# Sample attention beside expert lookups: VectorE's and ScalarE's stages set one pair of slots behind TensorE's, weights turned a stage later, joining products in another bank

## Chip, core and metric

The kernel is one program on one core of a Trainium2 chip. The metric is the device time of one execution in microseconds (us), the median over the runs. Names: TensorE (PE, its weight loads PEld), VectorE (DVE), ScalarE (ACT), GpSimd (POOL), SyncE (SP).

## What is computed

One inference step of a decoder of two layers, for a prompt of 512 rows and for eight sample rows that attend to a past of 4096 rows each. All is float32. Layer 0's first half is a convolution and a gated linear attention, layer 1's is multi-head latent attention; both layers end with an expert lookup (PEER). What matters here, cut from the reference:

```python
def odd_layer(x, pos, ckv_past, kpe_past, ...):       # layer 1: latent attention
    z = rms_norm(x, norm_g) @ w_in
    c_q, c_kv, k_pe = jnp.split(z, [R_Q, R_Q + R_KV], axis=-1)
    ...
    sp = (einsum('bqhr,bkr->bhqk', ql, ckv_past)      # sample rows: 8 sequences, 4096 past rows
          + einsum('bqhd,bkd->bhqk', qp, kpe_past)) * MLA_SCALE
    p = softmax(concatenate([sp, s], axis=-1))
    o = (einsum('bhqk,bkr->bqhr', p[..., :n_past], ckv_past) + einsum(... p[..., n_past:], ckv))
    ...
def peer(h, w_q, sub_keys, u_tab, v_tab):             # both layers: 8 heads, 16 experts of each
    q = (xf @ w_q).reshape(n, H_P, 2, D_HALF)
    s_top, i_top = top_k(einsum('nhcd,hckd->nhck', q, sub_keys), TOPK)
    ... ids, gates = the 16 best sums of pairs, their softmax
    act = gelu(einsum('td,thkd->thk', xb, u_tab[ib])) * gb
    return einsum('thk,thkd->td', act, v_tab[ib])
```

`ckv_past` is (8, 4096, 256) and `kpe_past` (8, 4096, 32), read from a paged cache through `page_table`.

## The kernel before, in words

**Expert slots.** `peer_layer` handles 512 (head, expert) slots of 128 rows in each layer, and eight more of the sample rows. For a slot GpSimd gathers 128 rows of 8 KB (line 1177) into one of `RING` = 8 buffers, VectorE forms the dot of each row's first half with the normalised input (`dot`, line 1569), ScalarE the gelu, the product with the gate and a diagonal matrix (`weigh`, lines 1297, 1299, 1303), and TensorE adds the row's second half, weighted by the diagonal, to `acc` (`experts`, line 1782). Then the buffer is free for the slot eight further on. Slots go in pairs (`GROUP` = 2), and eight pairs (`GROUPS`) make one head n of `NW` = 32. Between the pairs of a head each engine has the routing of head n + 2: queries before the head's first pair on TensorE (line 1717, for half of the heads), scores after its second and third (line 1727), their copies on ScalarE, the top-k on VectorE behind the dots of pairs 3 to 6.

**Attention beside them.** The latent attention of layer 1 is spread over both lookups, since its work fits between slots. It is written as generators, one per engine: `latent_round` for the prompt rows, then `sample_round` for the sample rows (sequences 0 and 1 beside layer 0's lookup, 2 to 7 beside layer 1's). Each engine chains the two and, at the end of every pair of slots, takes one step (`next(steps, None)`, lines 1147, 1197, 1408, 1663, 1834), in layer 0 from head 14 on, in layer 1 up to head 27; what is left runs after the last pair. So stage s of the attention stands, on every engine, behind the same pair's slot work. Engines are bound to each other by semaphores alone and each executes its list in order. `latent_round` has 93 stages in layer 0 and 101 in layer 1; the sample round has 51 and 118.

**A piece.** The past of a sequence is read in four pieces of 8 x 128 rows (1.18 MB). A piece p begins a new stage every four (`piece_at(s, offset)`). Its stages, with the engine's line: offset -2 the gather on GpSimd (line 2527, into one of three page buffers, after the weighted products of piece p - 3); 0 and 1 TensorE turns two quarters of the pages each (`turn_pages`, line 2802: left in bank 0, right in bank 1), ScalarE copies the left (line 2570) and the last right part (line 2574), VectorE the first right part (`page_out`, line 2653); 2 the rotary part (lines 2824 and 2578); 3 the scores (`scores`, lines 2850 and 2854, in bank 2), their maximum (`maxima`, line 2665) and exponentials (`exps`, lines 2583 and 2584); 4 the weights turned (`turn_weights`, line 2860, in bank 2) and copied (`weights_out`, line 2590); 5 the weighted products (`weighted`, line 2869, in bank 2) and their sum (`add_piece`, lines 2681 and 2688). Stage 4 of a piece is stage 0 of the next.

**Joins.** After a sequence's last piece four short steps join the partial sums: `turn_top`, `spread_top`, `total_sums` and `fold_heads` on TensorE (lines 2874, 2880, 2887, 2893) with `largest`, `shares`, `weighed_sum`, `normed` and `folded` (line 2720) on the others. They are four stages apart while pieces follow and one apart at the end of a round. Their products go to bank 2, which `scores` of the next piece may enter only once they are read (its last four waits). At layer 0's end VectorE adds `acc` to x (line 1584) behind the last pair.

Of the kernel before, what the change touches and what calls it, by code (L numbers as in the profile page):

```python
# [953 lines left out]
GROUP = 2  # L954
# [11 lines left out]
def peer_layer(nc, w, layer, ident, x_sb, smp, out):  # L966
# [11 lines left out]
    with ExitStack() as ctx:  # L978
# [81 lines left out]
        assert att["stages"] <= GROUPS * (NW - ROUND_AT if layer == 0 else PAIR_NORM)  # L1060
        assert att["stages"] + smp_att["stages"] <= GROUPS * (NW - ROUND_AT if layer == 0 else SMP_X)
        block = ctx.enter_context(nc.Block())
# [40 lines left out]

        def hooked(n):
            return n >= ROUND_AT if layer == 0 else n < SMP_X

        @block.sync
        def _(sp):
# [16 lines left out]
            for n in range(-AHEAD, NW):  # L1125
                i = head_of(n + AHEAD)
                for g in range(GROUPS):
                    if g == 4 and i is not None and n + AHEAD < NW and i + HEADS_IN < NQ_HEADS:
                        sp.wait_ge(s_ps, score_no(n + AHEAD + H_P) + 1)
                        if with_sample(i):  # L1130
                            sp.wait_ge(smp_s_ps, i % H_P + 1)
                        load_head(i + HEADS_IN)
                    if last_layer and n == SMP_X - 1 and g == 4:
                        sp.wait_ge(s_ps, score_no(NW - 1) + 1)
                        load_head(NQ_HEADS)
                        load_head(NQ_HEADS + 1)
                    if last_layer and n == SMP_X and g == 1:
                        sp.wait_ge(smp_att["done"], 1)
                        for h in range(HEADS_IN, H_P - 1):
                            w_dst, k_dst = smp_head(h)[0:2]  # L1140
                            sp.dma_start(w_dst, w["w_q_heads"][layer, :, h]).then_inc(smp_w_in, 16)
                            sp.dma_start(k_dst.rearrange("p c n -> p (c n)"), w["keysT"][layer][:, D_KEY * h:D_KEY * h + D_KEY]).then_inc(smp_w_in, 16)
                    if last_layer and n == SMP_HEADS and g == 2:
                        sp.wait_ge(smp_s_ps, 1)
                        sp.dma_start(w_q[:, 0], w["w_q_heads"][layer, :, H_P - 1]).then_inc(w_q_in[0], 16)
                        sp.dma_start(keys[:, 0].rearrange("p c n -> p (c n)"), w["keysT"][layer][:, D_KEY * (H_P - 1):D_KEY * H_P]).then_inc(w_q_in[0], 16)
                    if n >= 0 and hooked(n):
                        next(steps, None)
# [14 lines left out]
        def _(pool):  # L1163
# [22 lines left out]
            for n in range(NW):  # L1186
# [6 lines left out]
                for k in range(TOPK):  # L1193
                    if n == 0 and k == 8:
                        pool.wait_ge(routed, 1)
                    gather(first_slot(n) + k, ids[:, n % (AHEAD + 1), k:k + 1])
                    if hooked(n) and k % GROUP == GROUP - 1:
                        next(steps, None)
# [4 lines left out]
        def _(act):  # L1203
# [154 lines left out]
            for n in range(NW):  # L1358
# [6 lines left out]
                for g in range(GROUPS):  # L1365
# [40 lines left out]
                    if g == 6 and m < NW:  # L1406
                        exps(route_no(m))
                    if hooked(n):
                        next(steps, None)
# [9 lines left out]
        def _(dve):  # L1419
# [197 lines left out]
            for n in range(NW):  # L1617
# [6 lines left out]
                for g in range(GROUPS):  # L1624
# [26 lines left out]
                    if m < NW:  # L1651
# [9 lines left out]
                        if g == 6 + late:  # L1661
                            lookup(route_no(m), ids[:, m % (AHEAD + 1), :])
                    if hooked(n):
                        next(steps, None)
# [11 lines left out]
        def _(pe):  # L1676
# [125 lines left out]
            for n in range(NW):  # L1802
# [6 lines left out]
                for g in range(GROUPS):  # L1809
# [22 lines left out]
                    if (n, g) == SPREAD_PE[1]:  # L1832
                        smp_spread_x(1)
                    if hooked(n):
                        next(steps, None)
# [556 lines left out]
def sample_round(nc, ctx, w, out, ident, x_sb, smp, rnd, att):  # L2392
# [6 lines left out]
    LAST_AT = SETUP + 4 * (NPC - 1)  # L2399
    OUT_AT = LAST_AT + 11  # L2400
    STAGES = LAST_AT + 10 if rnd == 0 else OUT_AT + 7

# [54 lines left out]
    s_cols, o_cols = banks[2][:, 0:256], banks[2][:, 256:256 + R_KV]  # L2457
    top_row, bias_col, total_col, fold_out = banks[2][0:1, 0:128], banks[2][:, 0:1], banks[2][:, 0:1], banks[2][:, 0:2 * H_C]

# [8 lines left out]
    def merge_stage(i, step):  # L2468

        last = PAST_PIECES * i + PAST_PIECES - 1  # L2470
        return SETUP + 4 * last + 6 + step * (4 if last + 1 < NPC else 1)

# [5 lines left out]

    def outs_before(i, step):

        return min(PAST_PIECES * i + PAST_PIECES + step, NPC)

# [7 lines left out]
    def sync_steps(sp):  # L2490
# [10 lines left out]
        for s in range(STAGES):  # L2501
# [8 lines left out]
            if rnd == 1 and s == LAST_AT + 4:  # L2510
                sp.wait_ge(s_ps, NPC)
                sp.dma_start(w_uv, w["c_w_uv"][0].rearrange("(k p) h n -> p k (h n)", p=128)).then_inc(uv_in, 16)
            if rnd == 1 and s == LAST_AT + 6:
                sp.wait_ge(o_ps, NPC)
# [30 lines left out]
    def scalar_steps(act):  # L2545
# [46 lines left out]
        def shares(i):  # L2592
# [6 lines left out]
            nc.scalar.activation(share[:, 1:2], new_top(PAST_PIECES * i + PAST_PIECES - 1), ACT.Exp, bias=share[:, 0:1], scale=MLA_SCALE).then_inc(share_ready, 1)  # L2599

        for s in range(STAGES):
            if rnd == 0 and s == 6:
# [3 lines left out]
            if rnd == 0 and s == 8:  # L2606
                latent_queries_out()
            if (p := piece_at(s, 4)) is not None:
                weights_out(p)
# [16 lines left out]
    def vector_steps(dve):  # L2626
# [95 lines left out]
        def add_out():  # L2722
# [4 lines left out]
            last.then_inc(y_used, 1)  # L2727

        for s in range(STAGES):
            if rnd == 0 and s == 6:  # L2730
# [3 lines left out]
            if rnd == 0 and s == 9:  # L2734
                self_out()
            if (p := piece_at(s, 5)) is not None:
                add_piece(p)
# [18 lines left out]
    def tensor_steps(pe):  # L2756
# [48 lines left out]
        def turn_pages(p, r):  # L2805
# [10 lines left out]
            elif p:  # L2816
                pe.wait_ge(right_act, p)
            turn_page(banks[1], p, 4 * r + 2, right_ps)

# [7 lines left out]
        def scores(p):  # L2827
# [7 lines left out]
            elif rnd == 0:  # L2835
                pe.wait_ge(self_ready, 1)
            if p >= PAST_PIECES:
                i, step = divmod(p - PAST_PIECES, PAST_PIECES)
                if step == 0:
                    pe.wait_ge(mx_ready, i + 1)  # L2840
                if step == 1:
                    pe.wait_ge(bias_out, i + 1)
                if step == 2:
                    pe.wait_ge(inv_step, 2 * i + 1)
                if step == 3:
                    pe.wait_ge(olT_ready, i + 1)
            b = ROUND_SEQS[p // PAST_PIECES]
# [24 lines left out]
        def turn_top(i):  # L2872
            pe.wait_ge(o_used, outs_before(i, 0))
            nc.tensor.transpose(top_row, new_top(PAST_PIECES * i + PAST_PIECES - 1), ident[:]).then_inc(topT_ps, 1)

        def spread_top(i):
            pe.wait_ge(consts, 1)
            pe.wait_ge(nmx_ready, i + 1)
            pe.wait_ge(o_used, outs_before(i, 1))
            nc.tensor.matmul(bias_col, nmx[:].rearrange("p j h -> p (j h)"), one[:], start=True, stop=True).then_inc(bias_ps, 1)  # L2880

        def total_sums(i):
            pe.wait_ge(lw_ready, i + 1)
            pe.wait_ge(bias_out, i + 1)
            pe.wait_ge(consts_in, 48)
            pe.wait_ge(o_used, outs_before(i, 2))
            nc.tensor.matmul(total_col, fold[:], share[:, 2:3], start=True, stop=True).then_inc(total_ps, 1)

        def fold_heads(i):
            pe.wait_ge(on_ready, i + 1)  # L2890
            pe.wait_ge(o_used, outs_before(i, 3))
            for c in range(2):
# [22 lines left out]
        for s in range(STAGES):  # L2915
# [11 lines left out]
            if (p := piece_at(s, 2)) is not None:  # L2927
                turn_rope(p)
            if (p := piece_at(s, 4)) is not None:
                turn_weights(p)  # L2930
            if (p := piece_at(s, 5)) is not None:
                weighted(p)
# [127 lines left out]
```

## Time and profile before

| | us |
|---|---|
| median of 3 runs | 3596.35 (3595.26 to 3619.91) |
| the profiled execution | 3605.23 |
| its span, first to last instruction | 3603.4 |
| PE / DVE / ACT / POOL busy in the span | 2576.4 / 2175.5 / 1593.2 / 1195.2 |
| mean granted TensorE clock | 0.816 of full speed |
| moved | 1240.70 MB, mean 344 GB/s |

A row of the profile gives a line of the kernel, the engine, what it writes and reads, its duration, and in brackets how long the engine was idle before it and what released it. A wait is put down to what came last. Layer 0's lookup runs up to about 1846 us, layer 1's from about 1890 us.

### The profile page before, as it was taken

The page shows a single profiled execution, that of the slowest core. Times are in us where ns is not written, and L with a number is a line of the kernel's source. Part 1 is how long each engine was busy: PE and PEld are TensorE (multiplying, and loading weights), DVE is VectorE, ACT ScalarE, POOL GpSimd, SP SyncE. Part 2 cuts the span into 40 slices and gives each one's busy share as a digit, 9 for nine tenths or more (in the row PEclk, how much of TensorE's full clock was granted, in tenths as well). Part 3 has the DMA queues.
Part 4 walks back from the last instruction along what each step waited for, and adds up shares of the span by engine and source line. Part 5 has one row for each costly group of instructions (what it writes and reads, how often), then busy time and mean ns, then how long its engine had stood idle before and what let it go on. Part 6 is the DMA issues. An engine that isn't in the chain of part 4 may idle for free. (4 is left out here: it accounts for less than half of the span.)

```text
span 3603.4 us, 44291 instructions
## 1 busy us (share of the span) xinstructions
PE 2576.4 (71%) x15271; PEld 1136.2 (32%) x15271; DVE 2175.5 (60%) x5407; ACT 1593.2 (44%) x4435; POOL 1195.2 (33%) x1114
## 2 busy tenths in 40 slices
PE   8987776666788875766656888866767666656566
PEld 7644222111334432322232443422323322221121
DVE  4863667767776776545345778866454454455566
ACT  3122444444555663244433557744444444444344
POOL 0210444444443443333213344433222222222343
PEclk9988776766898997776777999988888778776687
DMA  4115999999999999898759999999888788888998
GB/s 158 46 32 190 411 426 426 422 427 427 418 400 421 422 420 396 359 370 308 278 214 384 408 421 421 423 406 368 328 330 302 288 309 304 294 295 314 417 426 362
DMA packets 215854, 1240.70 MB, mean 344 GB/s; under 512 B 28015, under 2 KB 63503, under 8 KB 72773
## 3 DMA queue, kind: packets, MB, share of 16 engines
q0 software_dynamic: 154368, 1128.34, 77.5%
q1 hardware_dynamic: 59965, 108.63, 8.2%
q8 instruction: 121, 1.98, 0.2%
q10 hardware_dynamic: 1296, 0.90, 0.1%
q14 instruction: 104, 0.85, 0.1%
HBM read 1233.79 MB, written 4.46 MB: 344 GB/s over the span
## 5 line engine op out<-in xcount | busy, mean ns | idle before, releaser
L1782 PE MATMUL p_acc<-p_rows,p_diag 64*64 64x512 f32 x8192 | 1390.5, 791 | 865.7 <-ACT p_diag L1303 850.3
L1177 POOL DMA_INDIRECT p_rows<-in_peer_uv,p_ids x1024 | 1102.3, 1076 | 2036.6 <-PE p_acc L1782 1886.7
L1569 DVE CUSTOM_DVE_ANT_0 p_rows<-p_rows,p_x_n 128x1024 f32<-128x1024 f32 x1040 | 1248.5, 1221 | 491.6 <-DMA p_rows<-in_peer_uv,p_ids 479.5
L1782 PEld LDWEIGHTS p_acc<-p_rows,p_diag 64*64 64x64 f32 x8192 | 288.3, 159 | 1655.2 <-ACT p_diag L1303 1477.5
L1297 ACT ACTIVATE p_acts<-p_dots 128x1 f32<-128x1 f32 x1040 | 209.2, 201 | 1038.7 <-DVE p_dots L1569 1035.0
L1303 ACT ACTIVATE p_diag<-p_unit,p_gated 128x64 f32<-128x64 f32 x1024 | 356.0, 348 | 33.5
L1299 ACT ACTIVATE p_gated<-p_acts,p_gates 128x1 f32<-128x1 f32 x1024 | 301.7, 295 | 33.3
L1717 PE MATMUL p_q_banks<-p_xT,p_w_q 128*128 128x256 f32 (+3 forms) x1152 | 245.0, 374 | 22.9 <-DMA p_keys<-in_keysT 14.5
L1717 PEld LDWEIGHTS p_q_banks<-p_xT,p_w_q 128*128 128x128 f32 x1152 | 210.1, 204 | 57.9 <-issue 30.9
L1297 ACT ACT_TABLE_LOAD x142 | 182.2, 1283 | 5.9 <-DVE p_dots L1569 3.4
L2665 DVE TENSOR_REDUCE s_peak<-r_bank 128x1 f32<-128x256 f32 x32 | 13.6, 424 | 178.3 <-PE r_bank L2854 178.3
L2653 DVE COPY r_arena<-r_bank 128x512 f32<-128x512 f32 x32 | 22.1, 691 | 145.3 <-PE r_bank L2802 145.3
L2802 PEld LDWEIGHTS r_bank<-ident,r_arena 128*128 128x128 f32 x512 | 81.0, 187 | 71.5 <-issue 71.5
L2688 DVE SCALAR_TENSOR_TENSOR r_arena<-r_arena,s_alpha,r_bank 128x256 f32<-128x256 f32 x32 | 15.4, 480 | 141.3 <-PE r_bank L2869 141.3
L2802 PE MATMUL r_bank<-ident,r_arena 128*128 128x128 f32 x512 | 96.4, 351 | 0.0
L541 DVE SCALAR_TENSOR_TENSOR a_conv<-a_u,a_conv_wc,a_conv 128x512 f32<-128x512 f32 x120 | 86.6, 793 | 0.0
L688 PE MATMUL a_ps<-a_xT,a_w_in 128*128 128x260 f32 x384 | 85.7, 384 | 0.1
L1569 DVE DVE_READ_ACCUMULATOR2_ANT p_dots<- 128x1 f32 x1040 | 84.5, 81 | 0.0
L1289 ACT ACT_TABLE_LOAD x64 | 82.1, 1283 | 1.1
L2355 PE MATMUL r_bank<-r_arena 128*128 128x256 f32 x192 | 52.9, 437 | 41.1 <-DMA r_arena<-in_c_w_out 41.1
L688 PEld LDWEIGHTS a_ps<-a_xT,a_w_in 128*128 128x128 f32 x384 | 72.6, 190 | 11.9 <-issue 0.4
L2570 ACT COPY r_arena<-r_bank 128x512 f32<-128x512 f32 x64 | 37.7, 588 | 83.2 <-PE r_bank L2802 83.1
(417 smaller groups left out, 2787.3 us busy)
## 6 DMA issues: line engine op xcount, KB each, us to landing
p_w_q<-in_w_q_heads SPq DMA_DIRECT2D x35, 1024.0 KB
p_rows<-in_peer_uv,p_ids POOLq DMA_INDIRECT x1024, 14.2
r_arena<-in_c_w_out SPq DMA_DIRECT2D x8, 1024.0 KB, 24.7
a_w_in<-in_ab_w_in SPq DMA_DIRECT2D x6, 1024.0 KB, 11.7
r_arena<-in_w_qx SPq DMA_DIRECT2D x16, 384.0 KB, 12.6
r_arena<-in_c_w_in SPq DMA_DIRECT2D x2, 2688.0 KB, 13.0
r_arena<-in_w_q_heads SPq DMA_DIRECT2D x5, 1024.0 KB, 23.8
p_keys<-in_keysT SPq DMA_DIRECT2D x35, 128.0 KB
```

Of the source, the lines that this page charges most:

```text
L541: ins = nc.vector.scalar_tensor_tensor(out=conv[:, c, 0:SEQ], in0=u[:, c, i:i + SEQ], scalar=conv_wc[:, c, i:i + 1], in1=conv[:, c, 0:SEQ] ...
L688: last = nc.tensor.matmul(ps[bank][:, 512 * b:512 * b + half], w_in[:, k, at:at + 128], xT[:, k, half_of(b)], start=(k == 0), stop=(k == K ...
L1177: nc.gpsimd.indirect_dma_start(out=rows[:, slot % RING, :], out_offset=None, in_=w[f"peer_uv{layer}"], in_offset=bass.IndirectOffsetOnAxis ...
L1289: nc.scalar.activation(ex[:], rel[:], ACT.Exp, accum_out=ex_sum[:]).then_inc(ex_ready, 1)
L1297: nc.scalar.activation(acts[:, i % 4, j:j + 1], dots[:, i % 4, j:j + 1], ACT.Gelu).then_inc(gelud, 1)
L1299: nc.scalar.mul(gated[:, i % 4, j:j + 1], acts[:, i % 4, j:j + 1], gate[:, j:j + 1]).then_inc(gated_ready, 1)
L1303: nc.scalar.mul(diag[:, i % 4, j, 0:n], unit[:], gated[:, i % 4, j:j + 1]).then_inc(diag_ready, 1)
L1569: nc.vector.tensor_tensor_reduce(rows[:, k % RING, 0:D_MODEL], rows[:, k % RING, 0:D_MODEL], x, 1.0, 0.0, ALU.mult, ALU.add, dots[:, slot ...
L1717: last = nc.tensor.matmul(q_banks[:, c, lo:hi], w_q[:, i % HEADS_IN, k, 128 * c:128 * c + 128], xT[:, k, lo:hi], start=(k == 0), stop=(k = ...
L1782: last = nc.tensor.matmul(acc[64 * c:64 * c + 64, 512 * r:512 * r + 512], diag[of, slot // GROUP % 4, j, :], rows[of, (slot + j) % RING, a ...
L2355: last = nc.tensor.matmul(banks[2 * (q % 2) + i][:, 0:256], oT[:, k, 128 * i:128 * i + 128], w_out[:, q % W_SLOTS, k, :], start=(k == 0), ...
L2802: last = nc.tensor.transpose(bank[:, 256 * c + 128 * u:256 * c + 128 * u + 128], past[:, p % PAGES, at:at + 128], ident[:])
```

## The change

In `sample_round`, VectorE's and ScalarE's generators begin with a bare `yield`, so that each of their stages stands one pair of slots behind TensorE's, SyncE's and GpSimd's. The stages from the turned weights on move up by one: weights turned and copied at offset 5, weighted and added at 6, the joins from offset 7 of the last piece. The joins' products go to bank 1 instead of bank 2: they wait for the right pages read (`right_act`) instead of `o_used`, and the right page turn waits for them to be read, instead of `scores`. `turn_top` waits for the maximum itself. `OUT_AT` goes up by one (119 stages in layer 1) and layer 0's round has 53 stages, of which the last two (and three on VectorE and ScalarE) run after the last pair. `hooked` takes a second argument that it does not use.

```diff
-        assert att["stages"] + smp_att["stages"] <= GROUPS * (NW - ROUND_AT if layer == 0 else SMP_X)
+        assert att["stages"] + smp_att["stages"] < (GROUPS * (NW - ROUND_AT) + 4 if layer == 0 else GROUPS * SMP_X)
...
-    OUT_AT = LAST_AT + 11
-    STAGES = LAST_AT + 10 if rnd == 0 else OUT_AT + 7
+    OUT_AT = LAST_AT + 12
+    STAGES = LAST_AT + 12 if rnd == 0 else OUT_AT + 7
...
-    top_row, bias_col, total_col, fold_out = banks[2][0:1, 0:128], banks[2][:, 0:1], banks[2][:, 0:1], banks[2][:, 0:2 * H_C]
+    top_row, bias_col, total_col, fold_out = banks[1][0:1, 0:128], banks[1][:, 0:1], banks[1][:, 0:1], banks[1][:, 0:2 * H_C]
...
-        return SETUP + 4 * last + 6 + step * (4 if last + 1 < NPC else 1)
+        return SETUP + 4 * last + 7 + step * (4 if last + 1 < NPC else 1)
...
-    def outs_before(i, step):
-
-        return min(PAST_PIECES * i + PAST_PIECES + step, NPC)
+    def turned_before(i, step):
+
+        return min(PAST_PIECES * i + PAST_PIECES + 1 + step, NPC)
...
-            if rnd == 1 and s == LAST_AT + 6:
+            if rnd == 1 and s == LAST_AT + 7:
                 sp.wait_ge(o_ps, NPC)
...
+        yield
         for s in range(STAGES):
...
-            if (p := piece_at(s, 4)) is not None:
+            if (p := piece_at(s, 5)) is not None:
                 weights_out(p)
...
+        yield
         for s in range(STAGES):
...
-            if (p := piece_at(s, 5)) is not None:
+            if (p := piece_at(s, 6)) is not None:
                 add_piece(p)
...
             elif p:
                 pe.wait_ge(right_act, p)
+            if r == 0 and p > PAST_PIECES:
+                i, step = divmod(p - PAST_PIECES - 1, PAST_PIECES)
+                if step == 0:
+                    pe.wait_ge(mx_ready, i + 1)
+                if step == 1:
+                    pe.wait_ge(bias_out, i + 1)
+                if step == 2:
+                    pe.wait_ge(inv_step, 2 * i + 1)
+                if step == 3:
+                    pe.wait_ge(olT_ready, i + 1)
             turn_page(banks[1], p, 4 * r + 2, right_ps)
...
-            if p >= PAST_PIECES:
-                i, step = divmod(p - PAST_PIECES, PAST_PIECES)
...
         def turn_top(i):
-            pe.wait_ge(o_used, outs_before(i, 0))
+            pe.wait_ge(top_step, 3 * (PAST_PIECES * i + PAST_PIECES))
+            pe.wait_ge(right_act, turned_before(i, 0))
...
-            pe.wait_ge(o_used, outs_before(i, 1))
+            pe.wait_ge(right_act, turned_before(i, 1))
...
-            if (p := piece_at(s, 4)) is not None:
+            if (p := piece_at(s, 5)) is not None:
                 turn_weights(p)
-            if (p := piece_at(s, 5)) is not None:
+            if (p := piece_at(s, 6)) is not None:
                 weighted(p)
```

`total_sums` and `fold_heads` wait for `right_act` in the same way, with steps 2 and 3.

## Rows read from the trace of the kernel before

**Rows 1.** The page's slices: GB/s in 40 equal slices of the span.

```profile
GB/s 158 46 32 190 411 426 426 422 427 427 418 400 421 422 420 396 359 370 308 278 214 384 408 421 421 423 406 368 328 330 302 288 309 304 294 295 314 417 426 362
```

**Rows 2.** Busy time by stretch: start:end, us, PE, PEld, DVE, ACT, POOL, clock, DMA share, GB/s.

```profile
1550.00:1810.00 260.00, 161.99 (x1081) 59.45 (x1073) 120.96 (x302) 111.38 (x299) 73.68 (x74) 0.73 0.83 314
2070.00:2320.00 250.00, 219.86 (x1310) 106.22 (x1303) 193.35 (x506) 159.39 (x417) 109.09 (x94) 0.96 1.02 421
2535.00:3307.00 772.00, 496.14 (x3480) 219.38 (x3476) 378.63 (x1009) 347.95 (x903) 208.24 (x213) 0.80 0.83 304
```

**Rows 3.** The same, of the dots (line 1569) alone.

```profile
1550.00:1810.00 260.00, 81.63 (x138) 0.73 0.83 314
2535.00:3307.00 772.00, 227.47 (x384) 0.80 0.83 304
```

**Rows 4.** Waits in layer 1's sample attention, then in layer 0's: total us, times, longest.

```profile
DVE s_peak L2665 <- PE r_bank L2854: 136.5, 24, 14.4
DVE r_arena L2653 <- PE r_bank L2802: 107.8, 23, 7.2
DVE r_arena L2688 <- PE r_bank L2869: 96.0, 24, 6.0
...
DVE s_peak L2665 <- PE r_bank L2854: 41.8, 8, 7.5
DVE r_arena L2653 <- PE r_bank L2802: 37.3, 8, 6.2
DVE r_arena L2688 <- PE r_bank L2869: 36.9, 7, 6.2
```

**Rows 5.** Waits in the stretch 2070 to 2320 us.

```profile
DVE p_rows L1569 <- DMA p_rows<-in_peer_uv,p_ids: 42.5, 37, 2.1
```

**Rows 6.** Timeline of one pair of slots, 2769 to 2779 us: start, us, engine, line.

```profile
2769.68 0.69 DVE L2653 COPY r_arena<-r_bank 128x512 f32<-128x512 f32 x1 [3.55 <-PE r_bank L2802]
...
2770.22 0.59 ACT L2570 COPY r_arena<-r_bank 128x512 f32<-128x512 f32 x1
...
2771.43 1.22 DVE L1569 CUSTOM_DVE_ANT_0 p_rows<-p_rows,p_x_n 128x1024 f32<-128x1024 f32 x1
...
2772.51 3.23 PE L1782 MATMUL p_acc<-p_rows,p_diag 64*64 64x512 f32 x16 [2.60 <-ACT p_diag L1303]
...
2778.19 0.48 DVE L2688 SCALAR_TENSOR_TENSOR r_arena<-r_arena,s_alpha,r_bank 128x256 f32<-128x256 f32 x1 [2.64 <-PE r_bank L2869]
```

**Rows 7.** Timeline of TensorE where it has the queries, 2783 to 2805 us.

```profile
2783.36 7.07 PE L1717 MATMUL p_q_banks<-p_xT,p_w_q 128*128 128x256 f32 x32
2790.36 1.95 PE L1782 MATMUL p_acc<-p_rows,p_diag 64*64 64x512 f32 x16
2792.24 1.07 PE L2850 MATMUL r_bank<-r_arena,smp_qlT 128*32 128x256 f32 x16
2793.12 0.62 PE L2854 MATMUL r_bank<-r_arena,s_qpb 128*32 128x128 f32 x16
2797.67 3.69 PE L1782 MATMUL p_acc<-p_rows,p_diag 64*64 64x512 f32 x16 [3.93 <-ACT p_diag L1303]
```

**Rows 8.** Transfers of layer 1's sample attention, then of 2070 to 2320 us.

```profile
DMA packets 33496, 235.01 MB, mean 304 GB/s; under 512 B 3665, under 2 KB 5073, under 8 KB 5626
p_rows<-in_peer_uv,p_ids POOLq DMA_INDIRECT x192, 7.6
r_arena<-in_cache_rows,smp_row_ids POOLq DMA_INDIRECT x21, 9.8
...
p_rows<-in_peer_uv,p_ids POOLq DMA_INDIRECT x94, 15.3
```

**Rows 9.** Timeline of the end of layer 0.

```profile
1842.94 1.03 PE L2893 MATMUL r_bank<-s_fold_h,r_arena 128*128 128x16 f32 x4
1844.01 0.21 DVE L2720 COPY smp_olT<-r_bank 128x32 f32<-128x32 f32 x1 [4.54 <-PE r_bank L2893]
1844.12 2.77 DVE L1584 TENSOR_TENSOR x_sb<-x_sb,p_acc 64x512 f32<-64x512 f32 x4
```

More of the change, by code:

```diff
@@ L1102, in buffer_of, with hooked @@
             return x_n[:, t % 3, :]
-        def hooked(n):
+        def hooked(n, g):
             return n >= ROUND_AT if layer == 0 else n < SMP_X
@@ L1146, in _ @@
                         sp.dma_start(keys[:, 0].rearrange("p c n -> p (c n)"), w["keysT"][layer][:, D_KEY * (H_P - 1):D_KEY * H_P]).then_inc(w_q_in[0], 16)
-                    if n >= 0 and hooked(n):
+                    if n >= 0 and hooked(n, g):
                         next(steps, None)
@@ L1196, in _ @@
                     gather(first_slot(n) + k, ids[:, n % (AHEAD + 1), k:k + 1])
-                    if hooked(n) and k % GROUP == GROUP - 1:
+                    if k % GROUP == GROUP - 1 and hooked(n, k // GROUP):
                         next(steps, None)
@@ L1407, in _ @@
                         exps(route_no(m))
-                    if hooked(n):
+                    if hooked(n, g):
                         next(steps, None)
@@ L1662, in _ @@
                             lookup(route_no(m), ids[:, m % (AHEAD + 1), :])
-                    if hooked(n):
+                    if hooked(n, g):
                         next(steps, None)
@@ L1833, in _ @@
                         smp_spread_x(1)
-                    if hooked(n):
+                    if hooked(n, g):
                         next(steps, None)
@@ L2836, in scores @@
                 pe.wait_ge(self_ready, 1)
-            if p >= PAST_PIECES:
-                i, step = divmod(p - PAST_PIECES, PAST_PIECES)
[L2839 to L2846, printed above, removed]
             b = ROUND_SEQS[p // PAST_PIECES]
@@ L2885, in total_sums @@
             pe.wait_ge(consts_in, 48)
-            pe.wait_ge(o_used, outs_before(i, 2))
+            pe.wait_ge(right_act, turned_before(i, 2))
             nc.tensor.matmul(total_col, fold[:], share[:, 2:3], start=True, stop=True).then_inc(total_ps, 1)
@@ L2890, in fold_heads @@
             pe.wait_ge(on_ready, i + 1)
-            pe.wait_ge(o_used, outs_before(i, 3))
+            pe.wait_ge(right_act, turned_before(i, 3))
             for c in range(2):
```

## The prediction, made before the changed kernel was run

> **What bounds the kernel now.** I read the slices of the page first, then the busy time by stretch, the waits, the transfers, and last a timeline of single steps. The whole program reads 1240.7 MB, and the slices show two levels [rows 1]: 420 to 427 GB/s in the middle of each layer, near 300 in slices 17 to 19 and 28 to 35. The low slices are where the sample attention runs. Its stretch in layer 1 (2535 to 3307 us, 24 pieces) and in layer 0 (1550 to 1810 us, 8 pieces) move 304 and 314 GB/s, the stretch of layer 1 just before, with another attention and the same expert work, 421 [rows 2]. The dots divide these into pairs of slots (each dot is a product and an accumulator read, so four instructions to a pair) [rows 3]: 384 make 96 pairs in 772 us, 8.04 us each; 138 make 34.5 in 260 us, 7.5 each. The fast stretch gathers 94 slots, 47 pairs, in 250 us [rows 8]: 5.3 each. No engine is full in the slow stretches: TensorE has 496 of 772 us, VectorE 379, ScalarE 348 [rows 2]. So latency bounds them, and the waits name it [rows 4]: VectorE waits 136.5 + 107.8 + 96.0 = 340.3 us for TensorE's scores, turned pages and weighted products, and 41.8 + 37.3 + 36.9 = 116.0 us in layer 0; it has no wait for rows near the top of either list. In the stretch before, it waits for the rows' DMA instead, 42.5 us [rows 5]: that is how a stretch looks that the transfers bound.
>
> The timeline shows the ring [rows 6]. The page copy on VectorE waits 3.55 us for turned pages and ends at 2770.4; only then come the two dots (1.22 us each, the second from 2771.43), ScalarE's gelu, gate and diagonal (the experts begin at 2772.51, 1.0 us behind the first dot's end), TensorE's 16 expert products (3.23 us), its turn, and again a copy that VectorE has waited for (2.64 us). TensorE does nothing from the end of one step to the next diagonal (2.60 us). Every engine waits once round the ring, and TensorE, paused so often, is granted 0.80 of its clock here against 0.96 in the fast stretch [rows 2]. The experts' 16 products took 1.95 us straight after seven busy microseconds of queries, and 3.69 us after the next pause of 3.93 us [rows 7], the two levels of 2.4 and 1.2 GHz.
>
> **The bare `yield` on ScalarE and VectorE.** Stage s of the sample attention then stands behind the dots (on ScalarE the gelus) of pair h + 1, where TensorE's stands behind its experts of pair h. It removes no instruction; it takes the wait out of the ring. While TensorE does experts and stage of pair h, VectorE already does the dots of h + 1. VectorE's list would be 772 - 340 = 432 us in layer 1 and 260 - 116 = 144 in layer 0, if each wait went. I checked each consumer on TensorE for a new wait. The bank for the next turn is emptied by ScalarE right behind the gelus of the same pair, a 0.59 us copy [rows 6] beside experts of 1.95 to 3.69 us; VectorE's copy (0.69) stands behind its dots and at most 2.9 us of routing, which end about when the experts do. Scores need the rotary copy of the same pair, likewise covered. VectorE's `add_piece` releases the score bank behind the dots of the pair in which TensorE wants it, 0.7 us against the same cover. If that cover goes, it costs about a microsecond a piece, 32 in all.
>
> **Weights turned and multiplied a stage later.** `exps` now runs on ScalarE a pair later; without the shift TensorE would meet it too early. Same instructions, no cost. But `weighted` frees the page buffer, and the gather of piece p + 3 stands two pairs ahead on GpSimd's queue. GpSimd runs four pairs ahead of the experts (8 row slots), so the gather's wait now falls on exactly the pair in which TensorE does `weighted`. Queued behind it are the row gathers; the next of them needs a slot that the experts after `weighted` free, so it would wait anyway. What stays is the gather's own issue, 1.0 to 1.9 us, at most 1 us late per piece beside a ring of four pairs: 0 on the path, and up to 32 us if rows are the bound with no slack.
>
> **Joins in bank 1.** They move out of the score bank, so `scores` drops its four waits and the right page turn takes them. The largest is step 1: the turn waits for ScalarE's bias copy, behind `exps`, which stands behind VectorE's routing and maxima. About 1.5 us for TensorE, once for each of eight sequences, under VectorE's list: nothing, at most 12 us.
>
> **What is late next.** The transfers. The 772 us stretch moves 235.01 MB [rows 8], at 422 GB/s 557 us, above VectorE's 432 and TensorE's 496 busy (fewer at a better clock). The worst pair, the one with the queries, blocks TensorE for 7.07 + 1.95 + 1.1 + 0.6 = 10.7 us [rows 7], and VectorE then stands at the maxima; but rows in flight (7.6 us to land here, 15.3 where transfers bound [rows 8]) span it. An octet of pairs with queries is then 10.7 us plus seven pairs at 3.5 to 5 (experts of 1.95 to 3.7 and a stage of 1.5), 35 to 46 us; VectorE's own list is 432 / 12 = 36; the transfers of an octet are 557 / 12 = 46. That is near enough that some gaps stay, so I take 400 GB/s rather than 422. Layer 1: 235.01 / 0.400 = 588, a gain of 184 us (bounds: 0, and 215 at 422). Layer 0: 260 x 0.314 = 81.6 MB, / 0.400 = 204, a gain of 56 (0 to 66). The joins at the end of layer 0 (1810 to 1846 us) have four more such waits, the last 4.54 us [rows 9]; half of it gone is 6 (0 to 18). Against that, layer 0 now has 53 stages from pair 93 on in 144, so its last fold and copy come after the last 2.77 us addition: 1.03 + 0.21 [rows 9] and the small norm steps, +2 us (0 to +5). Layer 1's tail keeps its length (-8 to +5, I take 0).
>
> The sum against the profiled execution, 3605.2 us outside a span of 3603.4: 3605.2 - 184 - 56 - 6 + 2 = 3361. It lies 8.9 us above the median of the runs, so the forecast is 3352 us.
>
> One rule speaks against this. The Trainium skill (DMA: Bandwidth & Descriptors, Where 436 GB/s comes from) holds that transfers from HBM are bound by a core's share of the stack, about 358 GB/s. By it the layer 1 stretch could not fall under 656 us and I would gain some 116 us there and 32 in layer 0. The trace disagrees: 421 GB/s stood for 250 us [rows 2], so it changes nothing in the sum.
>
> **Rivals.**
> *TensorE becomes the bound.* If the clock stays low, its 496 us at 0.80 stretch to 496 x 0.80 / 0.65 = 610, and with gaps of a tenth of a microsecond or so at each turn near 650; layer 0 162 to about 205. For: 0.73 in layer 0. Against: 0.96 where TensorE has 220 of 250 us. Gain 120 + 50 + 4: 3422 us.
> *The pages cap the transfers.* In the slow stretch a DMA share of 0.83 carried 304 GB/s, so a full one 370. Then 635 and 221 us: gain 137 + 39 + 4, 3416 us. Against: with page gathers among them the first slices of layer 0's stretch show 425 to 430.
> *It does not do what it says.* VectorE waits for TensorE's previous pair nearly as long, since the ring merely spans two pairs. If a quarter of 340 + 116 us goes: 114, 3482 us. Against: TensorE's half of the ring (experts and stage, 4 to 6 us) then overlaps all of VectorE's.
> *Slower: page gathers block GpSimd.* If the wait for `weighted` holds the row gathers back a full landing each time, 9.8 us [rows 8] x 32 pieces = 314 us against the 244: 3666 us with the rest unchanged. It decides from 7.6 us a piece. For: GpSimd is in order and its wait moves onto the path. Against: the argument above that the next row slot is freed only later.
>
> **How the numbers follow.** Forecast 0.63, TensorE 0.16, pages 0.09, little done 0.07, slower 0.04, the rest elsewhere. The likeliest alone spans 3310 to 3395. To 8 in 10 I add the two partial cases: 3300 (422 GB/s throughout, 215 + 66 + 18) to 3450. About 1% is what a measurement of this kernel tells from no change: faster by more 0.93, within 0.03, slower 0.04.
>
> **What would show it.** Right: the stretches of sample attention at 390 to 422 GB/s and 5.8 to 6.3 us a pair; VectorE's waits on the scores, page and product lines under 100 us together in layer 1, and waits on the rows' DMA in their place; rows landing in 11 to 16 us; a clock above 0.85. A clock of 0.7 with TensorE never idle would show the first rival, a full DMA share at 370 GB/s the second, waits of 250 us and more on those lines the third, GpSimd's page gather waiting for the weighted products with VectorE short of rows the last. A time above 3450 would make the argument wrong.

## The result, and the profile after

The changed kernel takes 3294.45 us (median of 4 runs, 3292.26 to 3296.81); the kernel before 3605.38 us, over four runs (the three of the table above and one more). The ratio is 0.9135, 95% interval 0.9096 to 0.9174: 311 us faster. The forecast was 3352 us with a range from 3300 to 3450. The direction was right, the gain was forecast too small: 244 us from 3596.35 us, and the time lies 6 us under the lower end of the range.

The page of the changed kernel, three of its rows of slices (40 slices of 82.3 us; they answer to [rows 1]):

```profile
PEclk9979777776789899886887898998889889887588
DMA  4022899999999999989997999999899999999998
GB/s 173 1 85 90 360 427 426 426 422 426 427 411 397 422 421 418 425 342 412 426 426 298 378 417 422 421 422 423 343 426 426 426 425 426 426 424 425 423 401 358
```

The two low plateaus are gone. From slice 29 to 37 there is one level, 423 to 426 GB/s (slices counted from 0). What is low now: the first four slices (layer 0's first half), 17, 21 and 22 (the change of layers), 28 and the last two. Slices 17 and 28 are where TensorE makes the prompt attention's output products (line 2355, 1409 to 2361 us), for whose weights it waits; the last experiment starts there.

The sample attention's stretches, layer 0 and layer 1, with the columns of [rows 2], and the dots of 400 us from the middle of layer 1, as [rows 3]:

```profile
1532.00:1752.00 220.00, 155.60 (x1245) 56.07 (x1244) 137.20 (x330) 110.38 (x328) 88.11 (x84) 0.83 0.99 416
2440.00:2997.00 557.00, 428.03 (x3504) 196.70 (x3496) 380.57 (x1009) 328.56 (x894) 243.50 (x216) 0.88 1.01 425
...
2500.00:2900.00 400.00, 165.02 (x273) 0.88 1.01 426
```

The 96 pairs of layer 1 took 772 us; now 1009 instructions of VectorE, the same as then, take 557. VectorE's busy time is the same (379 and 381 us), TensorE's fell from 496 to 428 us at the better clock (0.88 against 0.80). 273 / 4 is 68 pairs in 400 us, 5.9 us each.

The waits of the layer 1 stretch, then of layer 0's (answer to [rows 4]):

```profile
POOL p_rows L1177 <- PE p_acc L1782: 291.4, 125, 7.2
ACT p_acts L1297 <- DVE p_dots L1569: 184.1, 125, 4.1
PEld p_acc L1782 <- ACT p_diag L1303: 183.4, 129, 5.4
DVE p_rows L1569 <- DMA p_rows<-in_peer_uv,p_ids: 135.2, 93, 3.8
...
DVE s_peak L2666 <- PE r_bank L2856: 29.4, 9, 4.7
...
PE r_bank L2804 <- ACT s_share L2595: 5.6, 5, 1.9
...
DVE r_arena L2654 <- PE r_bank L2804: 0.5, 2, 0.3
POOL r_arena L2527 <- PE r_bank L2871: 0.3, 1, 0.3
...
POOL p_rows L1177 <- PE p_acc L1782: 109.1, 56, 7.5
...
DVE p_rows L1569 <- DMA p_rows<-in_peer_uv,p_ids: 72.9, 53, 7.7
```

VectorE's three waits for TensorE, 340 us before, are 29.4 us for the scores, 0.5 us for the pages and none for the products. In their place stands a wait for the rows' DMA, 135 us. The stretch now looks as the one of [rows 5] did. Its transfers:

```profile
DMA packets 33704, 236.90 MB, mean 425 GB/s; under 512 B 3703, under 2 KB 5111, under 8 KB 5543
...
p_rows<-in_peer_uv,p_ids POOLq DMA_INDIRECT x195, 16.8
...
r_arena<-in_cache_rows,smp_row_ids POOLq DMA_INDIRECT x21, 19.0
```

The bytes are nearly those of [rows 8] (236.90 against 235.01 MB). A row gather takes 16.8 us from issue to landing instead of 7.6, now that the rate is at the level of the fast stretch, where it took 15.3. One piece of the timeline, in order of time:

```profile
2641.62 1.07 PE L2871 MATMUL r_bank<-r_arena 128*32 128x256 f32 x16
...
2644.05 0.94 POOL L2527 DMA_INDIRECT r_arena<-in_cache_rows,smp_row_ids  x1 [0.30 <-issue]
2644.45 1.23 DVE L1569 CUSTOM_DVE_ANT_0 p_rows<-p_rows,p_x_n 128x1024 f32<-128x1024 f32 x1 [3.79 <-DMA p_rows<-in_peer_uv,p_ids]
...
2646.68 1.98 PE L1782 MATMUL p_acc<-p_rows,p_diag 64*64 64x512 f32 x8 [3.99 <-ACT p_diag L1303]
...
2650.38 0.48 DVE L2689 SCALAR_TENSOR_TENSOR r_arena<-r_arena,s_alpha,r_bank 128x256 f32<-128x256 f32 x1
```

VectorE waits 3.79 us for rows before a dot, and takes the weighted product at 2650.38 with no wait at all: it was made 8 us earlier. The page gather (line 2527) is issued 1.4 us after the end of the weighted products. Two row gathers stand before it on GpSimd, from 2641.57 to 2643.74 us, so it waited for its turn and not for the products.

Where the 311 us came from, by the time between the first diagonals (line 1303) of successive heads in the two traces:

| stretch | before | after | change |
|---|---|---|---|
| layer 0, heads 26 to 31 (sample pieces and joins) | 351.1 | 260.0 | -91.1 |
| last pair of layer 0 to first of layer 1 | 51.7 | 52.8 | +1.1 |
| layer 1, heads 11 to 13 | 155.9 | 149.8 | -6.1 |
| layer 1, heads 14 to 25 (sample pieces) | 779.1 | 556.4 | -222.7 |
| layer 1, heads 26 to 31 | 266.9 | 274.0 | +7.1 |

The last stretches of the two layers end with the last pair of the lookup. In layer 0, head 26 gave 10.1 us, heads 27 to 30 together 68.6 and head 31 12.5. Of the 6.1 us of heads 11 to 13, head 13 has 5.4: layer 1's first sample piece stands in it.

### The profile page after: what moved, and what is told of

Read it like the earlier page. It is cut to its first block and busy times, and to the rows that moved or that the text cites. A ratio compares the mean times of both kernels' runs of the same rounds, so it can differ in the third digit from the quotient of the medians.

```text
span 3292.7 us, 44278 instructions
## 1 busy us (share of the span) xinstructions
PE 2456.0 (75%) x15271; PEld 1094.4 (33%) x15271; DVE 2180.1 (66%) x5407; ACT 1560.1 (47%) x4416; POOL 1232.3 (37%) x1114
## 5 line engine op out<-in xcount | busy, mean ns | idle before, releaser
L1782 PE MATMUL p_acc<-p_rows,p_diag 64*64 64x512 f32 x8192 | 1293.5, 737 | 657.9 <-ACT p_diag L1303 643.2
L1177 POOL DMA_INDIRECT p_rows<-in_peer_uv,p_ids x1024 | 1144.4, 1118 | 1701.9 <-PE p_acc L1782 1533.9
L1782 PEld LDWEIGHTS p_acc<-p_rows,p_diag 64*64 64x64 f32 x8192 | 271.2, 151 | 1413.6 <-ACT p_diag L1303 1239.5
L2804 PE MATMUL r_bank<-ident,r_arena 128*128 128x128 f32 x512 | 75.0, 290 | 13.0 <-ACT s_share L2595 6.1
L2804 PEld LDWEIGHTS r_bank<-ident,r_arena 128*128 128x128 f32 x512 | 59.6, 148 | 64.2 <-issue 39.1
L2355 PEld LDWEIGHTS r_bank<-r_arena 128*128 128x128 f32 x192 | 41.2, 220 | 58.9 <-DMA r_arena<-in_c_w_out 45.8
L727 PE MATMUL a_ps<-a_w_in,a_xT 128*128 128x512 f32 x128 | 56.5, 597 | 0.9 <-DVE a_u L528 0.9
L1241 ACT COPY p_qT<-p_q_banks 128x512 f32<-128x512 f32 (+1 forms) x36 | 19.2, 533 | 79.2 <-PE p_q_banks L1717 79.1
L265 POOL TENSOR_TENSOR a_r<-a_r,a_head_gain 128x512 f32<-128x512 f32 x4 | 13.7, 3432 | 114.6 <-ACT a_r L339 114.6
## 6 DMA issues: line engine op xcount, KB each, us to landing
p_rows<-in_peer_uv,p_ids POOLq DMA_INDIRECT x1024, 15.3
p_keys<-in_keysT SPq DMA_DIRECT2D x35, 128.0 KB, 12.5
```

The costliest lines, as they stand in the source:

```text
L1177: nc.gpsimd.indirect_dma_start(out=rows[:, slot % RING, :], out_offset=None, in_=w[f"peer_uv{layer}"], in_offset=bass.IndirectOffsetOnAxis ...
L1782: last = nc.tensor.matmul(acc[64 * c:64 * c + 64, 512 * r:512 * r + 512], diag[of, slot // GROUP % 4, j, :], rows[of, (slot + j) % RING, a ...
L2355: last = nc.tensor.matmul(banks[2 * (q % 2) + i][:, 0:256], oT[:, k, 128 * i:128 * i + 128], w_out[:, q % W_SLOTS, k, :], start=(k == 0), ...
L2804: last = nc.tensor.transpose(bank[:, 256 * c + 128 * u:256 * c + 128 * u + 128], past[:, p % PAGES, at:at + 128], ident[:])
```

## The experiments

Each group of runs has its own runs of the kernel before, and these differ: medians of 3633.9, 3625.9, 3600.6 and 3630.5 us. So the gain of a variant is given against the median of its group, and variants that the transfers bound are also compared by their time.

**Which edit carries the gain.** `e1_no_lag` takes both bare yields out again, in `scalar_steps` and in `vector_steps`:

```diff
-        yield
         for s in range(STAGES):
```

> The changed kernel without its two bare yields: weights a stage later and joins in bank 1 stay. My theory (the lag alone takes the waits out of the ring; the other two edits only make room for it): 3590 to 3610 us, sample attention again near 300 GB/s, VectorE's waits on scores, pages and products 300 us or more in layer 1. Rival (the later weights or the other bank carry part of the gain themselves): under 3550 us.

Measured: 3639.0 us, ratio 1.0011 (0.9999 to 1.0023). The time is above the expected 3590 to 3610 us only as its group's kernel before is, at 3633.9. Its waits in the 772 us of [rows 4] (2535 to 3307 us):

```profile
DVE r_arena L2688 <- PE r_bank L2869: 173.3, 22, 9.9
DVE s_peak L2665 <- PE r_bank L2854: 139.8, 23, 14.6
...
DVE r_arena L2653 <- PE r_bank L2802: 87.7, 22, 6.9
```

They sum to 400.8 us, more than before the change (340 us), most of it on the weighted products (173.3 against 96.0 us). I take it that they now fall in a pair in which VectorE has less other work; that was not tested. The later weights and the other bank gain nothing by themselves; the whole gain needs the lag.

**Whose lag.** `e2_vector_lag_only` takes the yield out of `scalar_steps` alone, `e3_scalar_lag_only` out of `vector_steps` alone (there the copies of the queries and `shares` keep their old pair, as VectorE waits for them inside its own stage; the two further copies of the queries move likewise, from 7 to 6 and 8 to 7):

```diff
-            if rnd == 0 and s == 6:
+            if rnd == 0 and s == 5:
                 queries_out()
...
-            if (i := merge_at(s, 1)) is not None:
+            if (i := merge_at(s + 1, 1)) is not None:
                 shares(i)
```

> The lag on VectorE alone; ScalarE's stages stand beside TensorE's again. My theory: the ring is then TensorE's end of stage, ScalarE's copy (0.6 to 1.2 us), gelu to diagonal (0.9), experts, about 6.8 us a pair where the transfers need 5.8: 3400 to 3450 us, sample attention at 350 to 370 GB/s. Rival (VectorE's dots were the whole of the ring, ScalarE's waits beside it cost nothing): within 15 us of 3294.

> The lag on ScalarE alone, VectorE beside TensorE (the steps of the first queries and of the shares, for which VectorE waits within its stage, stay in their old pair). My theory: VectorE's copy still follows TensorE's turn and the dots follow it, so the ring has all its 2.4 us of dots and little goes: 3560 to 3600 us. Rival (ScalarE's waits are as much of the ring as VectorE's): 3450 or less.

Measured: VectorE's lag alone 3453.5 us, ratio 0.9506 (0.9481 to 0.9531), 180 us under its group's 3633.9; ScalarE's alone 3506.0 us, ratio 0.965 (0.9625 to 0.9675), 128 us under. The first misses its range by 3 us, with the rival far off. The second is a clear miss: 3560 to 3600 was expected, the rival said 3450 or less, and it fell between them. ScalarE's own waits were worth more than I gave them. The mean time from one pair's diagonal to the next, over layer 1's heads 15 to 24, shows how (us, by the pair's place in its head):

| | 0 | 1 | 2 | 3 | 4 | 5 | 6 | 7 | sum |
|---|---|---|---|---|---|---|---|---|---|
| before | 10.8 | 8.3 | 8.4 | 6.7 | 9.4 | 7.9 | 8.2 | 6.2 | 65.9 |
| no lag (`e1_no_lag`) | 11.2 | 8.0 | 6.7 | 7.0 | 10.1 | 7.6 | 8.9 | 8.2 | 67.7 |
| VectorE lags | 13.5 | 6.4 | 5.8 | 3.9 | 10.1 | 6.1 | 6.9 | 5.3 | 57.9 |
| ScalarE lags | 10.7 | 8.2 | 2.6 | 8.9 | 8.8 | 7.5 | 5.5 | 7.3 | 59.4 |
| both (the change) | 5.3 | 8.0 | 2.6 | 7.0 | 6.1 | 8.2 | 5.4 | 4.2 | 46.9 |

`e1_no_lag` is the kernel that differs from the two by one bare yield each. Against it, ScalarE's lag alone brings place 2 from 6.7 to 2.6 us and place 6 from 8.9 to 5.5. There VectorE has nothing to fetch from TensorE, and only ScalarE's copies had held the gelus back. In `e1_no_lag` VectorE has read the next pair's dots at 2827.3, and the gelu comes at 2830.06, behind a copy that waited 2.65 us for TensorE:

```profile
2827.19 0.08 DVE L1569 DVE_READ_ACCUMULATOR2_ANT p_dots<- 128x1 f32 x1
...
2828.84 0.37 ACT L2590 COPY r_arena<-r_bank 128x256 f32<-128x256 f32 x1 [2.65 <-PE r_bank L2860]
...
2830.06 0.23 ACT L1297 ACTIVATE p_acts<-p_dots 128x1 f32<-128x1 f32 x1
```

With ScalarE's lag:

```profile
2753.64 0.69 DVE L2654 COPY r_arena<-r_bank 128x512 f32<-128x512 f32 x1 [5.18 <-PE r_bank L2803]
...
2757.69 1.22 DVE L1569 CUSTOM_DVE_ANT_0 p_rows<-p_rows,p_x_n 128x1024 f32<-128x1024 f32 x1
2757.73 0.59 ACT L2570 COPY r_arena<-r_bank 128x512 f32<-128x512 f32 x1
2758.20 0.21 ACT L1297 ACTIVATE p_acts<-p_dots 128x1 f32<-128x1 f32 x1
```

VectorE still waits 5.18 us for the page, but ScalarE's copy at 2757.73 waits for nothing and the gelu follows at once. VectorE's lag alone gains most at place 3 (7.0 to 3.9 us) and place 7 (8.2 to 5.3). Place 0, with the queries, is 13.5 or 10.7 us with one lag and 5.3 only with both. So the ring had two gates, each in its own pairs.

The waits alone would not have told this. With VectorE's lag alone, the time falls by 180 us while VectorE's three waits over heads 14 to 25 are still 279 us, against 340 before:

```profile
DVE r_arena L2688 <- PE r_bank L2870: 106.4, 21, 8.0
DVE r_arena L2653 <- PE r_bank L2803: 102.1, 23, 6.8
DVE s_peak L2665 <- PE r_bank L2855: 70.9, 12, 8.5
```

ScalarE's copies wait 192.5 us for TensorE in the same stretch (lines 2570, 2578 and 2590), and the next pair's gelus stand behind them.

**The joins' bank.** `e4_joins_bank2` puts the joins back in bank 2 and their waits back on `scores`. TensorE's join steps 1 to 3 are changed as the one shown, and `turned_before` loses its `+ 1`. The lag then needs another order within a stage: VectorE's four join steps stand ahead of `maxima`, ScalarE's `shares` ahead of `exps`.

```diff
-    top_row, ... = banks[1][0:1, 0:128], ...
+    top_row, ... = banks[2][0:1, 0:128], ...
-            pe.wait_ge(right_act, turned_before(i, 0))
+            pe.wait_ge(o_used, turned_before(i, 0))
```

> The changed kernel with the joins' products back in bank 2 and their four waits back on the scores (on VectorE the join steps then stand before the maxima, on ScalarE the shares before the exponentials, or the engines would wait for each other). Each join then makes TensorE's scores wait for VectorE's step of the next pair, up to 4 us, 32 times. My theory (engines have slack, the transfers bound): 3295 to 3330 us. Rival (TensorE or the ring over two pairs is next to the bound, so each such wait counts): 3380 us or more.

Measured: 3297.1 us (3295.5 to 3302.4), ratio 0.9078 (0.906 to 0.9095). The waits came, in layer 1 up to 6.2 us each:

```profile
PE r_bank L2852 <- DVE smp_olT L2721: 25.2, 5, 5.7
PE r_bank L2852 <- ACT s_share L2595: 21.6, 5, 6.2
```

and cost nothing that can be told from the changed kernel's own spread (3291.3 to 3302.1 us over its two groups). The bank spares TensorE waits, not the kernel time, as long as the transfers bound it.

**The weights' stage.** `e5_weights_early` sets the weights back to offset 4 and the products to 5, with the lag kept (first `weights_out` and `turn_weights`, then `add_piece` and `weighted`):

```diff
-            if (p := piece_at(s, 5)) is not None:
+            if (p := piece_at(s, 4)) is not None:
-            if (p := piece_at(s, 6)) is not None:
+            if (p := piece_at(s, 5)) is not None:
```

> The changed kernel with the weights turned at offset 4 and multiplied at 5 again, the lag kept. TensorE then reaches the turning in the very pair in which ScalarE makes the exponentials, behind VectorE's routing, and waits up to 4 us for it, 32 times; nothing else moves. My theory (slack in the engines): 3295 to 3340 us, TensorE's waits for the exponentials in the trace. Rival (TensorE's order is on the path): 3294 + 32 x 4 = 3420 us.

Measured: 3297.8 us (3296.2 to 3301.3), ratio 0.9099 (0.9081 to 0.9116). The same again, and the wait itself was smaller than I had thought: in layer 1 six times, 6.8 us together.

```profile
PEld r_bank L2862 <- ACT r_arena L2584: 6.8, 6, 3.2
```

**Do the transfers bound it?** `e6_three_pages_new` and `e7_three_pages_old` gather only the first three pieces of each round; the later pieces read what lies in the buffers, so 26 page gathers are left out.

```diff
-            if p is not None and p >= PAGES:
-                gather_past(p)
...
-                pe.wait_ge(past_in[p % PAGES], 16 * (p // PAGES + 1))
+                pe.wait_ge(past_in[p % PAGES], 16)
```

> The changed kernel, but of each round's pages only the first three pieces are gathered, the later pieces reuse what lies in the buffers: 5 + 21 gathers of 1.18 MB left out, 31 MB, 72 us at 425 GB/s. My theory (the transfers bound the sample attention now): 3294 - 55 to 72, so 3222 to 3240 us, still above 415 GB/s. Rival (the engines' ring over two pairs is next to the bound): 3275 us or more, with the rate down to 370.

> The kernel before with the same 26 page gathers left out. My theory (before, latency bounded): the time stays within 1% of 3600 us. Rival (transfers took part already): 3540 us or less.

Measured: on the changed kernel 3228.6 us, 66 us less than 3294.45 (the group's own `e5_weights_early` had 3297.8); on the kernel before 3623.8 us, ratio 0.999 (0.9977 to 1.0003). 26 x 1.18 MB at 425 GB/s are 72 us, and 66 came back, at a rate of 419 GB/s still:

```profile
2450.00:2900.00 450.00, 370.87 (x3161) 178.82 (x3165) 341.12 (x911) 299.55 (x812) 202.22 (x173) 0.94 1.01 419
```

Before, the same bytes were free. This is the plainest evidence of what bounds each kernel. GpSimd loses the issue of these gathers too, about 1 us each, but GpSimd waited 291.4 us for free row buffers in the stretch of layer 1, so its own work was not what counted.

**How much room TensorE has.** `e8_turned_twice_new` and `e9_turned_twice_old` turn every page quarter twice:

```diff
         def turn_page(bank, p, slot, done):
-            for c in range(2):
+            for c in (0, 1, 0, 1):
```

> The changed kernel with every page quarter turned twice on TensorE: 32 pieces x 16 more transposes, 1.0 to 1.9 us for 8, so 64 to 120 us of TensorE. My theory (TensorE 77% busy in layer 1's stretch, slack): at most 40 us more, 3294 to 3335. Rival (TensorE next to the bound): 3370 or more.

> The kernel before with every page quarter turned twice on TensorE. My theory (before, TensorE's turning stood in the ring of waits): all of it shows, 32 pieces x 16 transposes, 60 to 120 us more than before. Rival (even before it was covered by something): under 20 us more.

Measured: on the changed kernel 3297.0 us (3295.8 to 3298.1), nothing; on the kernel before 3667.4 us against its group's 3600.6, 67 us more (ratio 1.0182, 1.0135 to 1.0229). TensorE was busy for 2576.4 us in the kernel before; the page of the old kernel with the double turns has

```profile
PE 2635.3 (72%) x15783; PEld 1199.2 (33%) x15783; DVE 2175.2 (59%) x5407; ACT 1596.0 (44%) x4435; POOL 1190.8 (32%) x1114
```

so 59 us more of TensorE cost 67 us of time there (49 to 82 by the interval, from two runs), and the same transposes, 47 us here (2456.0 to 2503.0), cost none.

**And VectorE.** `e12_vector_loaded` adds four reductions of a bank ahead of each page copy, their results unused:

```diff
+            for k in range(4):
+                nc.vector.tensor_reduce(extra[:, 4 * p + k:4 * p + k + 1], banks[1][:, :], AX.X, ALU.max)
             nc.vector.tensor_copy(pagesT[:, :, 2:4, :], ...)
```

> The changed kernel with four more reductions of a bank (128 x 512, about 0.6 us each) on VectorE ahead of each page copy: 32 x 4 x 0.6 = 77 us more of VectorE, results unused. If the slack is general (transfers bound and each engine has room): at most 20 us more, 3294 to 3315. Rival (VectorE's list, with the dots, is next to the bound, and its 400 GB/s allowance would have been due had it been any longer): 3340 or more.

Measured: 3299.9 us (3299.4 to 3300.4), 5 us over the changed kernel's 3294.45 and 2 us over its other median of 3298.2, for 71 us more of VectorE (2180.1 to 2250.9). The same 480 us of the changed kernel, then of this one:

```profile
2460.00:2940.00 480.00, 371.43 (x2991) 175.33 (x2991) 327.95 (x870) 283.73 (x768) 206.90 (x183) 0.88 1.01 425
```

```profile
2460.00:2940.00 480.00, 381.01 (x3053) 175.19 (x3045) 370.94 (x951) 282.39 (x765) 214.79 (x187) 0.89 1.01 423
...
DVE p_rows L1569 <- DMA p_rows<-in_peer_uv,p_ids: 19.5, 18, 2.1
```

VectorE is busy for 371 of 480 us instead of 328 and the rate only falls from 425 to 423 GB/s. But its wait for rows is down to 19.5 us in 400 (101.1 in the changed kernel): I read this as about all the room that it has; no run loaded it further.

**A further step.** In both kernels TensorE stands at the prompt attention's first output product for its weights (line 2355). `a0_changed_again` is the changed kernel unaltered; `e10_output_later_1_3` and `e11_output_later_3_3` move these products later, by one pair in layer 0 and three in layer 1 (shown), and by three in both, while the loads stay:

```diff
-    STAGES = HEADS_END + 4 + 10
+    LATER = 1 if rnd == 0 else 3
+    STAGES = HEADS_END + 4 + LATER + 10
...
-        i = s - HEADS_END - 4 - offset
+        i = s - HEADS_END - 4 - LATER - offset
```

> The changed kernel unaltered, for comparison on the same chip as the next runs: 3290 to 3300 us.

> A further step: the prompt attention's output products one pair later in layer 0 and three in layer 1, their weight loads where they were. In the changed kernel TensorE stands some 15 us at the first of them for a load that takes about 24 us in a full queue, and the transfers run dry behind it. My theory: layer 1 gains 10 to 14 us, layer 0 3 to 5: 3277 to 3283 us. Rival (the gap only moves, since the loads must pass the same queue anyway): within 4 us of the changed kernel.

> The same with three pairs in both layers; in layer 0 the last joins then run behind the last pair. My theory: layer 0's stall goes as well (10 to 15 us) and the uncovered joins give back 3 to 6: 3268 to 3278 us. Rival (uncovered joins cost as much as the stall): not below the version with one and three.

Measured in one group: 3298.2 us (3291.3 to 3302.1), 3289.8 (3284.9 to 3296.5), 3285.1 (3284.3 to 3286.7); ratios 0.9161 (0.9128 to 0.9194), 0.9138 (0.9103 to 0.9173), 0.9122 (0.909 to 0.9154). The first step was expected at 3277 to 3283 us and misses that; its runs overlap with the changed kernel's, so its gain is not settled. The second lies under every run of the changed kernel, though the intervals of the ratios overlap, and is the fastest: 13 us under the changed kernel by the medians of the group. It was expected at 3268 to 3278 us, 20 to 30 us under that median, and misses too. The wait for the weights, in the changed kernel and then in `e11`:

```profile
PE r_bank L2355 <- DMA r_arena<-in_c_w_out: 40.7, 4, 11.3
```

```profile
PE r_bank L2356 <- DMA r_arena<-in_c_w_out: 26.1, 3, 13.0
```

It is 15 us shorter, and three waits of up to 13 us remain. In layer 1 heads 11 to 13 went from 149.8 to 143.7 us, but head 12 alone rose from 50.7 to 55.8. I read this as the loads of the third and fourth quarter, which wait for a product before they start and so moved with it; that was not tested.

## Why the mechanism was right and the size was not

**The step that failed: the size of what is late next.** The prediction took the transfers to bound the changed kernel, which was right, at 400 GB/s "rather than 422", for gaps between pairs that differ in length. The layer 1 stretch ran at 425 GB/s, with every slice of it above 410. The term for layer 1 was 184 us, at 422 GB/s it was 215, and it measured 223 by heads 14 to 25. The eight pairs of a head had been put at 35 to 46 us by what TensorE does in them and at 46 by the transfers; they took 46.9 (heads 15 to 24), the transfers' time, so nothing was due for gaps. I read the full rate as the work of eight row buffers, which level out pairs of 2.6 to 8.2 us, and of the room that each engine has (TensorE for 47 us more, VectorE for 71, as measured); another number of buffers was not tried.

**Layer 0: the term was mis-sized by its stretch as well.** I counted 56 us from 1550 us on (66 at 422 GB/s), and 6 for the joins at its end; heads 26 to 31 gave 91. Heads 27 to 30 gave 68.6 us of it, about what the full rate allows. Head 26 (1489 to 1545 us), in which the first pieces already stand, was left out, 10.1 us; and head 31 gave 12.5 where I had 6 for the joins, within the bound of 18.

**Why the time lies even under the lower end.** That end had the full rate and all of the joins: 215 + 66 + 18 = 299 us of gain, 3297 us, stated as 3300. The stretches of the table gave 311.7. The 13 us more are 8 in layer 1's heads 14 to 25, 7 in layer 0's heads 26 to 31 (with head 26 in it) and 6 in heads 11 to 13, less 8 that the two ends gave back. The prediction also took 8.9 us off for the median of three runs. Over four runs the median of the kernel before is 3605.38, as in the profile, so this term had no ground; it moved the forecast and the lower end towards the result by luck.

**What bounded the kernel: right.** The ring of waits through all engines was the bound in the sample attention: VectorE's waits of [rows 4] went from 340 us to 30, and the runs with pages left out show that bytes were free before and cost nearly their full time after. Two of the signs that I named were missed narrowly: rows landed in 16.8 us instead of 11 to 16, and the clock was 0.88 in layer 1's stretch but 0.83 in layer 0's, under 0.85.

**The lag takes the waits out of the ring: right, and it is the only edit that gains.** Without it the other two edits give 1.0011. The covers that I named held: adding a copy's work, a wait for a join or a wait for exponentials changed nothing. What I did not see is how the two engines share the gain. I argued from VectorE's waits alone; ScalarE's lag is worth 128 us without VectorE's. The trace of the kernel before had the sign: ScalarE's copies waited 200.6 us for TensorE in layer 1's stretch, and none of these lines is left in the changed kernel's.

```profile
ACT r_arena L2590 <- PE r_bank L2860: 109.7, 24, 5.4
...
ACT r_arena L2570 <- PE r_bank L2802: 50.3, 22, 3.4
ACT r_arena L2578 <- PE r_bank L2824: 40.6, 23, 3.2
```

**Weights later, joins in bank 1: right at nothing**, by `e4` and `e5`. The wait of the right page turn for ScalarE's bias copy, which I bounded at 1.5 us each and 12 in all, was 5.6 us in layer 1, at most 1.9 each. Without the edit the scores wait longer than `e4` expected, up to 6.2 us, but these waits are covered too.

**The page gather behind `weighted`: right.** GpSimd's waits for the weighted products in layer 1 are a single 0.3 us. The slower rival is refuted.

**The small terms.** The joins behind layer 0's last pair: +2 us expected, +1.1 us between the layers. The timeline shows the 2.1 us after the addition:

```profile
1754.13 2.78 DVE L1584 TENSOR_TENSOR x_sb<-x_sb,p_acc 64x512 f32<-64x512 f32 x4
...
1757.34 0.35 DVE L2717 TENSOR_SCALAR r_arena<-r_arena,s_share 128x256 f32<-128x256 f32 x1
...
1757.75 1.04 PE L2896 MATMUL r_bank<-s_fold_h,r_arena 128*128 128x16 f32 x4 [3.09 <-DVE r_arena L2717]
1758.82 0.21 DVE L2721 COPY smp_olT<-r_bank 128x32 f32<-128x32 f32 x1 [1.13 <-PE r_bank L2896]
```

Layer 1's heads 26 to 31, taken at 0, gave back 7 us, 2 more than the bound of +5. Head 26 alone rose from 41.8 to 46.9 us. The end of the sample attention now stands in it, later by the lag and one stage, and its loads meet a queue that is already full; which of the two it is was not tested.

**The rivals.** TensorE was not the bound (0.88 of its clock, and free double turns); by its own stretches of 650 and 205 us its gain was 122 + 55 + 4, 3415 us, not 3422. The pages do not cap the transfers at 370 GB/s: with 21 page gathers in it the stretch ran at 425. The argument that I had against this rival was not one: the slices of 423 to 430 GB/s lie between 1550 and 1589 us, and the trace of the kernel before has no page gather from 1535 to 1605 us. Nor do page gathers make the share of 0.83 at 304 GB/s. In `e7_three_pages_old`, without them, the same stretch has 0.73 at 263 GB/s, so about 360 GB/s to a full share either way (304 / 0.83 is 366):

```profile
2535.00:3307.00 772.00, 494.35 (x3413) 216.82 (x3405) 364.09 (x972) 337.75 (x874) 175.67 (x186) 0.78 0.73 263
```

By the rows above, the stretch's 425 GB/s stood for 557 us. The rule of the Trainium skill that was weighed before the run (DMA: Bandwidth & Descriptors, Where 436 GB/s comes from), about 358 GB/s for a core, disagrees with that.

## What to carry to other kernels

Where engines work through lists in order and one engine's stage waits for another's of the same step, look for the wait that stands ahead of the next step's first work, and let the waiting engine's stage stand one step later; take every engine that waits, since each may be its own gate. Before sizing the gain, find what is late next, and size it for the whole stretch that the change touches, its first and last steps included, at the rate that this resource has shown in a saturated stretch; take something off for gaps only if a row shows them. And once one resource bounds, taking an edit out tells little by the time: here the waits moved and the time did not. Extra work on an engine tells how much room it has.

## What the runs showed that I had not expected

A DMA share does not scale to a ceiling: 0.83 with 304 GB/s before, 0.73 with 263 without the pages, 1.01 with 425 after. And the kernel before varied between groups of runs from 3600.6 to 3633.9 us, 0.9%, while the changed kernel and the variants that only load its engines lay between 3294.5 and 3299.9. The groups ran on different chips. If waits between engines vary more from chip to chip than the transfer rate does, that would explain it, but no run isolates it.
